# Three parts per Hyena tile between the attention units of layer 0

## The reference: two layers, and the attention of the first

```
s = einsum('bhmqd,bhmkd->bhmqk', qi, k) * scale     # m = 0, 1: two score maps per head
p = softmax(s)
w = p[:, :, 0] - lam * p[:, :, 1]
o = einsum('bhqk,bhkd->bhqd', w, v)
...
y_b = hyena_branch(z[..., COL_HY:COL_GB], ...)      # its columns of z = h @ w_in[l]
sh, sc, gt = modulation(c, ada_w[l], ada_b[l])      # silu(c) @ ada_w + ada_b, for x and for ctx
```

## Time and profile before

| | |
|---|---|
| three executions | 1659.42, 1666.4, 1672.19 us |
| the profiled execution's own time | 1662.07 us |
| its span, first to last instruction | 1660.8 us |
| TensorE matmul busy | 1533.5 us, 92% of the span |
| VectorE, ScalarE busy | 892.7 us (54%), 671.6 us (40%) |
| mean granted TensorE clock | 0.960 |

### The profile page before, as it was taken

One profiled execution on the slowest core, in us unless ns is written; L12 is line 12 of the kernel. 1 busy time (PEld: TensorE's weight loads), 2 busy tenths in 40 slices (PEclk: granted clock), 3 DMA queues, 4 the chain that ended last, 5 costly groups with the idle time before them and its releaser, 6 DMA issues.

```text
span 1660.8 us, 22235 instructions
## 1 busy us (share of the span) xinstructions
PE 1533.5 (92%) x9066; PEld 1279.7 (77%) x9066; DVE 892.7 (54%) x1573; ACT 671.6 (40%) x1174; POOL 32.5 (2%) x42
## 2 busy tenths in 40 slices
PE   5999989978999999969888999979989998999998
PEld 1587657756888887638677899968778778999997
DVE  3626653655533335565675765666543446766547
ACT  3423443033322224343453444556444343644434
POOL 0000000000000000100000000010000000200000
PEclk9899998999999999979999999989988999999999
DMA  7421332133332322233121455525321113555552
GB/s 290 166 101 62 117 141 75 51 111 134 104 103 89 102 89 96 89 107 110 63 101 61 164 201 186 175 99 193 133 94 63 40 55 126 187 180 181 190 188 77
DMA packets 57846, 203.14 MB, mean 122 GB/s; under 512 B 6256, under 2 KB 9456, under 8 KB 57616
## 3 DMA queue, kind: packets, MB, share of 16 engines
q1 hardware_dynamic: 55568, 194.01, 33.8%
q0 software_dynamic: 1888, 7.12, 1.2%
q10 hardware_dynamic: 288, 0.58, 0.1%
HBM read 200.65 MB, written 1.05 MB: 121 GB/s over the span
## 4 chain that ended last, share of the span: by engine, by line
PE 81%; DVE 11%; ACT 4%; DMA 2%; issue 1%; SPq 0%; ACTq 0%; DVEq 0%
PE gemm_bank L362 16%; PE gemm_bank L363 15%; PE gemm_bank L364 15%; PE misc_bank L362 6%; PE misc_bank L363 6%; PE misc_bank L364 6%; DVE wlo L1361 2%; PE misc_bank L804 2%; PE misc_bank L511 1%; PE misc_bank L817 1%; DMA raw<-in_stream 1%; PE misc_bank L714 1%; PE misc_bank L707 1%; DMA x<-in_ctx 1%; PE misc_bank L569 1%
## 5 line engine op out<-in xcount | busy, mean ns | idle before, releaser
L362 PE MATMUL gemm_bank<-hhi,wlo 128*128 128x256 f32 (+1 forms) x1328 | 442.1, 333 | 41.6 <-DVE wlo L1361 20.6
L1361 DVE TENSOR_TENSOR wlo<-raw,whi 128x1024 fp32r<-128x1024 f32 x316 | 381.3, 1219 | 111.5 <-ACT whi L946 107.5
L363 PE MATMUL gemm_bank<-hlo,whi 128*128 128x256 f32 (+1 forms) x1328 | 427.4, 322 | 0.0
L364 PE MATMUL gemm_bank<-hhi,whi 128*128 128x256 f32 (+1 forms) x1328 | 426.6, 321 | 0.0
L946 ACT ACTIVATE whi<-raw 128x1024 fp32r<-128x1024 f32 x316 | 332.1, 1052 | 179.9 <-PE gemm_bank L364 118.9
L362 PEld LDWEIGHTS gemm_bank<-hhi,wlo 128*128 128x128 f32 x1328 | 262.9, 198 | 73.5 <-DVE wlo L1361 24.8
L363 PEld LDWEIGHTS gemm_bank<-hlo,whi 128*128 128x128 f32 x1328 | 263.5, 198 | 15.6 <-issue 0.7
L364 PEld LDWEIGHTS gemm_bank<-hhi,whi 128*128 128x128 f32 x1328 | 262.4, 198 | 16.5
L362 PE MATMUL misc_bank<-hhi,wlo 128*128 128x256 f32 (+1 forms) x560 | 178.8, 319 | 0.0
L363 PE MATMUL misc_bank<-hlo,whi 128*128 128x256 f32 (+1 forms) x560 | 178.8, 319 | 0.0
L364 PE MATMUL misc_bank<-hhi,whi 128*128 128x256 f32 (+1 forms) x560 | 178.8, 319 | 0.0
(11 more groups left out here) (325 smaller groups left out, 1987.8 us busy)
## 6 DMA issues: line engine op xcount, KB each, us to landing
raw<-in_stream SPq DMA_DIRECT2D x364, 512.0 KB, 3.5
const_b<-in_const_b POOLq DMA_DIRECT2D x1, 1100.0 KB, 8.8
x<-in_x SPq DMA_DIRECT2D x1, 1024.0 KB, 11.3
x<-in_ctx SPq DMA_DIRECT2D x1, 1024.0 KB, 16.2
y<-in_hy_decay POOLq DMA_DIRECT2D x2, 512.0 KB, 6.9
arena<-in_gm_ws POOLq DMA_DIRECT2D x2, 512.0 KB, 5.6
y<-in_hy_w POOLq DMA_DIRECT2D x2, 256.0 KB, 4.9
shared<-in_dft POOLq DMA_DIRECT2D x1, 512.0 KB, 10.3
```

Of the source, the lines that this page charges most:

```text
L362: mm(out, w_lo, r_hi, start=first, stop=False)
L363: mm(out, w_hi, r_lo, start=False, stop=False)
L364: return mm(out, w_hi, r_hi, start=False, stop=last)
L1361: dve.tensor_tensor(self.wlo[:, t % SPLIT, :], self.raw[:, t % RAW, :], self.whi[:, t % SPLIT, :].bitcast(F32), ALU.subtract).then_inc(*se ...
```

## The change

Each Hyena tile's eight k-steps are cut in parts of two, four and two (`PARTS`). The first part stands ahead of the scores in the even unit, the second ahead of the scores in the odd unit, and the third behind the odd unit's turning, ahead of PV. The two modulation tiles move from behind the odd unit's turning to ahead of it, directly behind the scores. The row turning of units 4, 8 and 12 moves from ahead of the scores to behind the unit's turning. On ScalarE the next Hyena tile's `whi` moves to the head of the even unit, and the tile's own evacuation to behind the odd unit's exponentials. On VectorE the next tile's `wlo` stays in the odd unit, and the evacuation of the tile moves to the next even unit, behind its maxima.

```diff
--- before.py
+++ after.py
@@ -26,6 +26,7 @@
 SPLIT = 4
 AHEAD = 2
 AHEAD_HI = 3
+PARTS = (0, 2, 6, 8)
 FILL = [1] * 8, [0, 1, 0, 1, 0, 1, 0, 0]
 LN_FILL = [[3, 3, 3, 3], [2, 2]]
 D_FF = 2816
@@ -369,18 +370,17 @@
             self.pe.wait_ge(*self.at("evac", use - 4))
         return self.G[use % 4]
 
-    def pe_half(self, second):
-
-        T, s = self.tiles[self.pe_next], self.tiles[self.pe_next].t % SPLIT
-        if not second:
+    def pe_part(self, T, part):
+
+        s = T.t % SPLIT
+        if part == 0:
             self.pe.wait_ge(*self.at("tile_lo", T.t))
             self.pe_bank(T.use)
-        for k in range(4 * second, 4 * second + 4):
+        for k in range(PARTS[part], PARTS[part + 1]):
             c = slice(k * P, (k + 1) * P)
             m = self.three(self.G[T.use % 4][:, 0:T.n], self.whi[:, s, c], self.wlo[:, s, c], self.hhi[:, k, 0:T.n], self.hlo[:, k, 0:T.n], k == 0, k == KT - 1)
-        if second:
+        if part == 2:
             m.then_inc(*self.mark("tile_used", "used", T.t))
-            self.pe_next += 1
 
     def pe_feature(self, T, bank, hi, lo, begun=None, col=0):
 
@@ -634,18 +634,25 @@
             if l:
                 self.pe_tiles(FILL[0][u])
             else:
-                self.pe_half(u % 2)
-            if l == 0 and u in (4, 8, 12):
-                self.pe_turn(*self.LATE_ADA[u // 4 - 1])
+                T = self.tiles[self.pe_next]
+                self.pe_part(T, u % 2)
             if u + 1 < n:
                 self.pe_scores(l, u + 1)
+            if l == 0 and u % 2:
+                self.pe_next += 1
+                self.pe_tiles(2)
             pe.wait_ge(*self.at("weights", l, u))
             if u:
                 pe.wait_ge(*self.at("wt", l, u - 1))
             for kt in range(nkt):
                 m = pe.transpose(self.M[2][:, kt * P:(kt + 1) * P], self.tmp[:, 2, kt * P:(kt + 1) * P], self.ident)
             m.then_inc(*self.mark("pe_att", "w_turned", l, u))
-            self.pe_tiles(FILL[1][u] if l else 2 * (u % 2))
+            if l:
+                self.pe_tiles(FILL[1][u])
+            elif u % 2:
+                self.pe_part(T, 2)
+            elif u in (4, 8, 12):
+                self.pe_turn(*self.LATE_ADA[u // 4 - 1])
             if i == 1:
                 pe.wait_ge(*self.at("wt", l, u))
                 if u == 1:
@@ -1104,12 +1111,19 @@
         for u in range(n):
             (q_off, k_off, nkeys), h, i = units[u]
             nkt = nkeys // P
-            self.act_tiles(FILL[0][u] if l else u % 2)
+            if l:
+                self.act_tiles(FILL[0][u])
+            elif u % 2 == 0:
+                self.act_hi()
             act.wait_ge(*self.at("w_turned", l, u))
             act.activation(self.wt[:, 0:nkt, i * P:(i + 1) * P], self.M[2][:, 0:nkt * P].rearrange("p (k q) -> p k q", k=nkt), ACT.Copy).then_inc(*self.mark("act_att", "wt", l, u))
             if u + 1 < n:
                 self.act_exps(l, u + 1)
-            self.act_tiles(FILL[1][u] if l else 2 * (u % 2))
+            if l:
+                self.act_tiles(FILL[1][u])
+            elif u % 2:
+                self.act_tiles(1, split=False)
+                self.act_tiles(2)
             if i == 1:
                 act.wait_ge(*self.at("pv", l, u))
                 act.activation(self.y[:, h, q_off:q_off + TOK], self.M[3][:, 0:TOK], ACT.Copy).then_inc(*self.mark("act_att", "pv_out", l, u))
@@ -1586,13 +1600,21 @@
                 self.dve_tiles(FILL[0][u])
             if u + 1 < n:
                 self.dve_maxima(l, u + 1)
-            self.dve_tiles(FILL[1][u] if l else 3 * (u % 2))
+            if l:
+                self.dve_tiles(FILL[1][u])
+            elif u % 2:
+                self.dve_lo()
+                self.dve_lo()
+            elif u:
+                self.dve_tiles(2, split=False)
+                self.dve_tiles(1)
             if l == 0 and u in (4, 8, 12):
                 self.dve_turned(*self.LATE_ADA[u // 4 - 1])
                 if u == 8:
                     self.dve_mod_gate(0)
         if l == 0:
-            self.dve_tiles(1)
+            self.dve_tiles(2, split=False)
+            self.dve_tiles(2)
             self.dve_turned(*self.LATE_ADA[3])
         nt = TOK if l else ALL
         v.wait_ge(*self.at("head_root", l))
```

## The result

Over 20 executions of each the changed kernel takes 1654.17 us (1644.63 to 1663.08) and the kernel before 1662.97 us (1655.27 to 1672.19); the ratio is 0.9939, with a 95% interval from 0.9924 to 0.9954. That is 0.6% less: beyond doubt, and under the 1% that I had called tellable. The forecast was -3.25 us. Measured are 8.8 us between the medians, and 7.6 to 12.6 by the interval. The time itself, 1654.17 us, still lies in the stated range of 1654 to 1671, at its very edge. The gain is larger than any that the prediction's faster cases gave (8.0 us).

A forecast was written before the change was run, and what follows sets the result against it. TensorE was taken to bound the kernel, with only idle time to win. The terms -5.9 - 1.35 + 1.5 + 2.5 = -3.25 us took the median from 1666.4 to 1663.2 us; range 1654 to 1671.

The forecast's parts named there:

- the prediction's faster cases: Outcomes below the forecast: the shift ends a low-clock stretch, 1658.4 us, or the cut is free, 1660.6 us.
- The bound: TensorE bounds the stage from 149 to 257 us; a new order can give back only its idle time, 7.8 us.
- The wait for `wlo`: TensorE's seven waits for `wlo` ahead of the next Hyena tile all go: -5.9 us.
- The third cut: One more cut of the Hyena matmuls in each of eight pairs costs 0.31 us each: +2.5 us.
- the sign that the prediction set: In the profile after, three Hyena parts together taking 6.18 us would say that the cut costs 0.31 us.
- The first rival: The cut of the Hyena matmuls is free, as starts in a run do not wait for ends: -5.75 us, 1660.6; chance 0.15.
- The wait for the weights: TensorE's waits for weights ahead of turnings go, except 0.45 us in unit 0: -1.35 us.
- The first unit: The shorter first part leaves TensorE idle ahead of the next scores until the exponentials are done, once: +1.5 us.
- Covers: The third part's six matmuls, 1.62 us, replace the modulation tiles over the `wt` copy of 0.60 us: cost 0.
- the tight place in the even unit: Even unit's scores to odd unit's: 4.42 us of TensorE work, exponentials done with 0.26 spare; cost 0 or up to 0.4 a pair.
- ScalarE's head: At the even unit's head `whi` precedes the `wt` copy; a DMA landing within 6.9 us of the modulation matmuls costs 0.

The follow-up runs named there:

- e1: Kernel before with only `wlo` of the next Hyena tile moved ahead of the two evacuation steps on VectorE; stage 96.41 us against 104.32, ratio 0.994.
- e8: Kernel before with `wlo` of the next Hyena tile placed between the two evacuation steps on VectorE; stage 99.61 us, ratio 0.9971.
- e12: Changed kernel with the first part cut once more, around the even unit's scores, in all pairs but the first; stage 95.24 us, one execution.
- e2: Kernel before with only the two modulation tiles moved ahead of the odd unit's turning; stage 104.24 us, ratio 0.9999.
- e3: Changed kernel with two parts of four k-steps and no third, nothing between the odd turning and PV; stage 100.27 us, ratio 0.996 to the kernel before.
- e9: Changed kernel with ScalarE's `whi` of the next Hyena tile put back at the head of the odd unit; stage 94.93 us, ratio 0.9943 to the kernel before.
- e7: Changed kernel with the two modulation tiles put back behind the odd unit's turning, ahead of the third part; stage 99.06 us, ratio 0.9974 to the kernel before.
- e4: Changed kernel with the first pair's Hyena tile cut three, four and one k-steps; stage 94.79 us, 1654.35 us, ratio 0.9938 to the kernel before.
- e6: Changed kernel with the first part cut once more, around the even unit's scores, in every pair; stage 96.94 us, ratio 0.9949 to the kernel before.

## Why the prediction was wrong, step by step

- **The bound: wrong.** The prediction said: "all that a new order of the same instructions can give back is its idle time: 108.00 - 100.18 = 7.8 us". The stage gave back 9.4, and still has 1.9 us of idle time in unit 0. Busy time by modelled ends contains part of each wait: PV's row is 1.99 us long in e1 as in the earlier trace rows, while the next tile can start 1.65 us behind its start, or 1.54. The Trainium skill, "Trainium Kernel Development and Optimization" (Performance Expectations, on reading a trace), calls matmul busy time a bad metric because matmuls are pipelined; the trace agrees, with 1.99 against 1.54 to 1.65, and the earlier trace rows should have been read so.
- **The wait for `wlo`: mechanism right, size wrong by 2.6 us.** "All 5.9 us go" took the idle time shown for the cost. The eight waits cost 8.5 us: seven are some 0.35 us longer than shown, and the eighth, 0.19, was not shown at all. e1 and e8 show it with TensorE's order untouched.
- **The third cut: wrong by 3.2 us, the largest miss.** The forecast was +2.5 us, 0.31 in each pair. By the sign that the prediction set, the three parts take 1.65 + 2.94 + 1.46 = 6.05 us instead of 6.18, so a cut shows as 0.17 in the Hyena matmuls, and these grew by 1.6 us in all. What the sum left out is that the neighbours got shorter: PV by 0.9 us, the turning by 1.2 and the row turning by 0.2. Together that is -0.7 us where +2.5 was forecast. The sum had carried 0.59 us for the turning and 1.99 for PV into the new order, from rows with other neighbours; they took 0.41 and 1.54. One more cut by itself is 0.04 us (e12). The estimate came from 5.88 against 5.57 us, two runs of twelve against one of 24 that starts behind a wait. Without a wait that one takes 5.65 us (e1), so 0.1 of the 0.31 was the wait's.
- **The first rival.** The prediction had set the Trainium skill's rule, "TensorE: Matmul & The Clock Gate" (Part 2, step by step), against its own estimate: the drain of one matmul overlaps the filling of the next. "Whatever follows" was the prediction's own reading of it. A free cut gave the better size here, by 0.04 us in e12 and by the sum over the neighbours, and the first rival came nearer than the forecast. By its -5.75 it fell short as well, for the `wlo` waits and the neighbours.
- **The wait for the weights.** Forecast -1.35, measured -1.7: 1.46 in the distances of the scores and 0.24 in unit 15. That these waits could be added to the others was right only because both were removed: e2 shows that alone they were worth nothing.
- **The first unit.** Forecast +1.5, measured 1.49.
- **Covers.** The third part over the `wt` copy held (e3), as did the tight place in the even unit: no other scores waited.
- **ScalarE's head.** "A landing within 6.9 us costs nothing" held for 512 keys only. With 256 keys PV is 0.68 instead of 1.54 and the scores 0.63 instead of 1.06, so that the room is 0.2 + 1.5 + 0.7 + 1.7 + 0.6 = 4.7 us, beside landings of 3.5 to 6.3. In unit 10 `whi` could start only 217.40 - 212.28 = 5.1 us behind the modulation matmuls, beyond that room, and only the slack of the exponentials held it, by 0.4 us (0.25 in unit 15). It cost nothing in the changed kernel (e9), 0.9 us in e7 and 0.25 in e4.

The sum with the measured sizes: -8.5 - 0.9 (`wlo`, PV's neighbours) - 1.7 (weights) - 1.2 - 0.2 (turning, row turning) + 1.5 (unit 0) + 1.6 (Hyena matmuls) = -9.4 us. What stays open is why the turning and PV take less time beside Hyena matmuls than beside modulation matmuls.

## What to carry to other kernels

Measure a wait of TensorE from start to start, against the same pair of instructions where nothing was waited for; here the idle time shown was too low in every pair, and a place that shows none can wait too. Take a length for the new order from a row with the same neighbours: here the neighbours moved the stage by more than the cut that was being priced. Before adding up two waits of one loop, ask which one would still set the pace if the other were gone. Work out a margin for the shortest form of the loop, not for the form in the rows at hand.

## What the runs showed of the hardware

- After an idle time of 2.18 us in the first pair, the granted clock fell to 0.50, the 1.2 GHz level, for some 3 us (e6, one execution), and the scores took 2.00 us instead of 1.06. After 1.49 us of idle time in the changed kernel it stayed at 1.00.
- Cutting a Hyena tile's group once more, behind its first k-step and around scores that go to another bank, made the stage 0.04 us longer per pair (e12).
- A group of eight PV matmuls with a modelled length of 1.99 us lets the next matmul start 1.65 us behind its start (e1). With six Hyena matmuls ahead of it the row is 1.89 us long and the distance 1.54 (the changed kernel).
- A turning of two matmuls takes 0.37 us with the modulation matmuls behind it and 0.19 with Hyena matmuls behind it; one of four takes 0.59 and 0.41. No wait is shown in either.
